# Eight of the 31 taps of one convolution chunk computed on GpSimd instead of VectorE, in a fused decoder-layer kernel

## The reference

```
h = rms_norm(x, g_pre_mix) * (1 + sc1) + sh1
proj = h @ w_in                                  # (2048, 1024) @ (1024, 3072)
cv, cg, q, f, i, g = split(proj)                 # 512 columns each
y_conv = conv_module(cv, cg, ...)                # below
y_rec  = hgrn2(q, f, i, g, ...)                  # chunkwise gated recurrence
x = x + gt1 * rms_norm(concat(y_conv, y_rec) @ w_out, g_post_mix)
... then the router, 32 experts (top 2 of one group) and a second residual

def conv_module(val, gate, dw_kernel, dw_bias, ln_gain, ln_bias):
    u = val * sigmoid(gate)
    u = depthwise causal conv, width 31 (u, dw_kernel) + dw_bias
    return silu(layer_norm(u, ln_gain, ln_bias))
```

## Time and profile before

| | us |
|---|---|
| median of 3 runs (1734.64, 1740.06, 1742.0) | 1740.06 |
| the profiled execution | 1742.48 |
| its span, first to last instruction | 1740.4 |
| mixer: the four blocks and their steps | about 0 to 1115 |
| projections of blocks 1, 2, 3 | about 341 to 478, 581 to 718, 823 to 960 |

### The profile page before, as it was taken

The page is one execution under the profiler, slowest core; times in us unless marked ns, Lnnn a source line. Parts: engine busy times, 40 slices in busy tenths (PEclk is TensorE's granted clock), DMA queues, the critical chain, the costliest instruction groups (busy, mean ns, idle before and its releaser), DMA issues. The chain is left out here.

```text
span 1740.4 us, 23975 instructions
## 1 busy us (share of the span) xinstructions
PE 1536.9 (88%) x7445; PEld 1164.5 (67%) x7446; DVE 1245.5 (72%) x1981; ACT 857.4 (49%) x1495; POOL 380.8 (22%) x401
## 2 busy tenths in 40 slices
PE   2699987999999999999999999459899999999950
PEld 2589975688946789766889565346576666677630
DVE  4589666469885498965598844486678877877828
ACT  2323262333384423563233523216678778878835
POOL 1000000100001000011000011234366666666630
PEclk9999867999999999999999998659899999999985
DMA  9342334233233332332331323637999998789859
GB/s 330 110 145 97 97 121 170 73 85 97 86 109 98 92 98 89 121 105 78 85 97 50 133 85 97 190 127 231 347 324 316 318 330 253 221 248 315 257 107 361
DMA packets 200421, 291.25 MB, mean 167 GB/s; under 512 B 10559, under 2 KB 158172, under 8 KB 200347
## 3 DMA queue, kind: packets, MB, share of 16 engines
q1 hardware_dynamic: 170720, 197.15, 33.9%
q0 software_dynamic: 29360, 92.99, 19.3%
q10 hardware_dynamic: 266, 0.14, 0.0%
HBM read 240.42 MB, written 59.26 MB: 172 GB/s over the span
## 5 line engine op out<-in xcount | busy, mean ns | idle before, releaser
L930 DVE SCALAR_TENSOR_TENSOR cv<-u,taps,cv 128x512 f32<-128x512 f32 x480 | 321.8, 747 | 0.1
L1757 DVE TENSOR_TENSOR w_rest<-wgu,w_high 128x1024 fp32r<-128x1024 f32 x192 | 233.9, 1223 | 95.1 <-ACT w_high L1682 92.5
L1682 ACT ACTIVATE w_high<-wgu 128x1024 fp32r x192 | 201.4, 1054 | 140.0 <-PE pgu L1632 81.4
L484 PE MATMUL bank<-wo,yT 128*128 128x512 f32 x512 | 227.7, 601 | 2.5 <-ACT hT L660 2.5
L457 PE MATMUL bank<-hT_high,tiles_operand 128*128 128x512 f32 x512 | 201.2, 393 | 9.8 <-DVE hT_operand L903 8.5
L458 PE MATMUL bank<-hT_operand,tiles_operand 128*128 128x512 f32 x512 | 200.3, 391 | 0.0
L459 PE MATMUL bank<-hT_high,win_operand 128*128 128x512 f32 x512 | 200.2, 391 | 0.0
L484 PEld LDWEIGHTS bank<-wo,yT 128*128 128x128 f32 x512 | 97.1, 193 | 118.8 <-issue 118.8
L1642 PE MATMUL py<-wd,hTe 128*128 x384 | 172.6, 592 | 0.9 <-ACT yb L1709 0.9
L1630 PE MATMUL pgu<-w_high,x_high 128*128 128x512 f32 x384 | 155.4, 405 | 0.0
L1631 PE MATMUL pgu<-w_rest,x_high 128*128 128x512 f32 x384 | 151.1, 393 | 0.0
(11 more groups left out here) (330 smaller groups left out, 2873.8 us busy)
## 6 DMA issues: line engine op xcount, KB each, us to landing
win<-w_in_in SPq DMA_DIRECT2D x64, 512.0 KB, 5.1
wgu<-w_gate_in SPq DMA_DIRECT2D x32, 1024.0 KB
wgu<-w_up_in SPq DMA_DIRECT2D x32, 1024.0 KB
wd<-w_down_in SPq DMA_DIRECT2D x32, 1024.0 KB
win<-w_in_in SPq DMA_DIRECT2D x16, 1024.0 KB, 5.1
wo<-w_ada_in POOLq DMA_DIRECT2D x6, 2048.0 KB, 9.8
y_dram<-zeros POOLq DMA_DIRECT2D x17, 512.0 KB, 5.1
tiles<-x_in POOLq DMA_DIRECT2D x16, 512.0 KB, 5.8
```

The costliest lines, as they stand in the source:

```text
L484: last = nc.tensor.matmul(out[:], yT[:, w % 2, k, :], wo[:, k, half * 512:(half + 1) * 512], start=(k == 0), stop=(k == KD - 1))
L930: ins = V.scalar_tensor_tensor(out=cv[:, j], in0=u[:, j, w:w + T], scalar=tap, in1=cv[:, j], op0=ALU.mult, op1=ALU.add)
L1682: A(w_high[:, QK * q:QK * q + QK, :], c.wgu[:, bass.ds(slot, 1), QK * q:QK * q + QK, :].rearrange("p a k n -> p (a k) n"), ACT.Copy).then_ ...
L1757: V.tensor_tensor(w_rest[:, part, :], c.wgu[:, bass.ds(slot, 1), part, :].rearrange("p a k n -> p (a k) n"), w_high[:, part, :].bitcast(F3 ...
```

## The change

In the last chunk (j = 3) the taps w = 23 to 30, eight of its 31, are taken out of DVE's stream. POOL computes their sum into `tmp` in a new function `side_taps`: the first tap as a `tensor_scalar` into `tmp`, each of the other seven as a `tensor_scalar` into `scr` and a `tensor_tensor` add of `scr` into `tmp`. That is 15 POOL instructions a block, each waiting on `side_step` for the one before. They begin when all four chunks of this block's `u` are ready. At the end of `conv` DVE waits for `side_step` and adds `tmp` to chunk 3 of `cv`.

```
+        SIDE, SIDE_STEPS = 8, 15
+        CONV_STEPS, MASK_STEPS = NCH * CW - SIDE + 1 + 2 * NCH, 10
...
+            def side_taps(t):
+
+                ch = Chain(pool, side_step, t * SIDE_STEPS)
+                pool.wait_ge(u_ready, (t + 1) * NCH)
+                wait(pool, o_ms, t * NT)
+                wait(pool, dstate_ready, t * 2 * NT)
+                for w in range(CW - SIDE, CW):
+                    tap = c.taps[:, (NCH - 1) * CW + w:(NCH - 1) * CW + w + 1]
+                    out = tmp[:] if w == CW - SIDE else scr[:, 0:T]
+                    ch.link(nc.gpsimd.tensor_scalar(out, u[:, NCH - 1, w:w + T], tap, None, ALU.mult))
+                    if w > CW - SIDE:
+                        ch.link(nc.gpsimd.tensor_tensor(tmp[:], tmp[:], scr[:, 0:T], ALU.add))
+                assert ch.n == SIDE_STEPS
...
             load_ada(pool, 8)
+            side_taps(0)
             for n, p in enumerate((9, 4, 5)):
...
             for t in range(NB + 1):
+                if 0 < t < NB:
+                    side_taps(t)
                 store(t, [w for w in range(NT) if present("y", (w,), t)])
...
                         for j in pair:
+                            if j == NCH - 1 and w >= CW - SIDE:
+                                continue
...
                 taps((2, 3), 17, CW)
-                ch.sync()
+                dve.wait_ge(side_step, (t + 1) * SIDE_STEPS)
+                dve.wait_ge(conv_step, done[NCH - 1])
+                ch.link(V.tensor_tensor(cv[:, NCH - 1], cv[:, NCH - 1], tmp[:], ALU.add))
```

More of the change, by code:

```diff
@@ L154, in mixer_phase @@
         hT_raw, hT_split, high_ready, rest_ready = (sem("hT_raw0"), sem("hT_raw1")), sem("hT_split"), sem("high_ready"), sem("rest_ready")
-        proj_ready = sem("proj_ready")
+        proj_ready, side_step = sem("proj_ready"), sem("side_step")
         gate_sig, u_ready = sem("gate_sig"), sem("u_ready")
@@ L173, in mixer_phase @@
             sem(n) for n in ("conv_step", "q_gated", "ke_ready", "y_normed", "diff_ready"))
-        CONV_STEPS, MASK_STEPS = NCH * CW + 2 * NCH, 10
+        SIDE, SIDE_STEPS = 8, 15
+        CONV_STEPS, MASK_STEPS = NCH * CW - SIDE + 1 + 2 * NCH, 10
         block = ctx.enter_context(nc.Block())
```

## The result

| | before | after |
|---|---|---|
| median | 1741.03 us (4 runs, 1734.64 to 1747.23) | 1780.1 us (4 runs, 1771.02 to 1784.34) |
| the profiled execution's span | 1740.4 us | 1769.3 us |

The ratio is 1.0218, 95% interval 1.0163 to 1.0273: 2.2% slower, about 39 us. The forecast was 1787 in a range from 1753 to 1814, with a chance of 0.87 for slower. The profiled execution of after is the shortest of its four.

The account below looks back on a forecast made before the run. PE was taken to bound the mixer. DVE's loss of 14.1 us a block, less 2.25 (2.38 in block 0) absorbed, gives 47.3 us, minus 0 gain: 1789.8 from the profiled execution, 1787 against the median; range 1753 to 1814.

Parts of the forecast that it names:

- The bound and the two gates: In the projections PE bounds; DVE reaches it through each piece's split and the convolution's end; 2.25 us of delay is absorbed.
- the 6.20 us of idle time: DVE's idle time ahead of piece 10's split in block 2: no cushion, since DVE caused it one round trip earlier.
- The gate of block 0: In block 0 the narrowest late gate was taken to be the split of piece 8, with 2.38 us to spare.
- The gain of 0: At the convolution's end DVE saves 3.7 us, but ACT and DMA hold that place: 0 to 0.3 us a block, taken as 0.
- The loss: POOL's instructions exclude DVE's taps: 8 x 0.74 + 7 x 1.17, so DVE loses 14.1 us in a block.
- The one-input term: Hold of one POOL tensor_scalar of 512 columns, from a selection's row at 1.45 ns a column: 0.74 us, eight a block.
- PE's waits of 11 to 12 us a block: Expected sign in the projections of the profile after: PE waiting on DVE's split of a piece, 11 to 12 us a block.
- The cycle: One POOL hold and one or two taps in turn; 15 take 24 to 34 us, all before the head gates.
- rival (a): DVE keeps the port, POOL advances only in DVE's idle spots, and DVE waits at the add: 15 us, 1755; chance 0.13.
- Rival (b): Taps are exempt from contention and POOL runs beside DVE: 1739 to 1740, not slower; chance 0.11.
- Rival (c), the clock: PE standing in pieces 6 to 10 may drop to 1.2 GHz: up to some 15 us more, 1800; no separate chance.
- My 47: Predicted standing PE over all four blocks: 35.6 us in blocks 1 to 3 plus 11.7 in block 0, 47.3 us.

Follow-up runs that it names:

- the runs with 2 and 4 taps: The changed kernel with GpSimd taking only the last 2 or 4 taps of chunk 3 instead of 8: 1743.32 us and 1749.0 us.
- the VectorE-only kernel: The kernel before with 16 more taps in VectorE's stream, written to tiles nobody reads, GpSimd idle as before: 1774.01 us.
- the kernel with fills: Against the kernel before, VectorE keeps all taps and GpSimd does 15 fills a block that read nothing, instead of arithmetic: 1739.63 us.
- the last experiment: Against the kernel before, VectorE keeps all taps and GpSimd's 15 added instructions a block are all tensor_scalar, results unused: 1757.84 us.
- the first experiment: Against the kernel before, VectorE keeps all 31 taps, GpSimd does its 15 instructions a block and its sum is thrown away: 1776.37 us.

## Why the prediction was right, and where its sizes were off

**The bound and the two gates** held. PE's waits stand at splits of pieces, and the cushion of 2.25 us, made of two idle spots and 0.58 us ahead of piece 10, is what the runs with 2 and 4 taps bracket in blocks 1 to 3: 1.9 us of loss is free, 4.8 us costs 2.3 a block. Reading the 6.20 us of idle time as an echo and not as room was the step that carried the sum. Taken as room, it would have set 8.5 us against 10.8 of loss, and left about 2.3 us a block instead of the 8.4 that PE was late at piece 10. The gate of block 0 was misread: not piece 8 with 2.38 us, but piece 6 with 0.93 and piece 7 with 1.65. With all the loss ahead of piece 7, that is 0.7 us more in the sum.

**The gain of 0** held. DVE's 3.7 us showed as a wait for ACT, 5.11 us in the changed kernel and 3.98 with the taps left out, and the kernel with all taps back on DVE was no slower (1776.4 and 1780.1).

**The loss** had the right mechanism and the wrong size. I took 8 x 0.74 + 7 x 1.17 = 14.1 us; it is 8 x 0.43 + 7 x 1.03 = 10.7. The two-input term was near. The one-input term was taken from the length of a selection, less a fixed part; but a `tensor_scalar` takes 1.56 us alone and holds a tap for only 0.43, so its length says nothing of it. The nearer number would have been the fill's, 0.84 ns a column, times 512: 0.43 us, but only the runs show that. With both measured terms the sum is 10.7 x 4 - 9.1 = 34 us. PE's waits of 11 to 12 us a block, which were named as a sign, were 6 in block 2: 8.4 by this smaller loss, and a part of it went into slow work instead of waiting (below).

**The cycle** was right, 24 to 34 us for the 15: they took 645.85 to 674.95, 29 us. That is also the end of rival (a). POOL gets in at the next change-over between two DVE instructions (its longest two in block 2, 2.93 and 3.48 us, had met a split), and nobody waits at the add. Rival (b), exempt taps, fell with the first tap of 1.78 us.

**Rival (c), the clock,** is a real part, not an alternative. The windows of the changed kernel around the waits for pieces 6 and 10:

```profile
664.00:668.60 4.60, 2.14 (x10) 1.44 (x8) 4.60 (x4) 2.40 (x2) 4.42 (x3) 1.00 0.27 69
668.60:672.00 3.40, 3.35 (x8) 2.68 (x9) 3.40 (x4) 0.00 (x0) 3.22 (x3) 0.50 0.62 215
716.00:719.10 3.10, 0.00 (x0) 0.00 (x0) 2.29 (x2) 3.10 (x4) 0.00 (x0) 1.00 0.59 166
719.80:723.20 3.40, 3.40 (x18) 3.40 (x18) 3.40 (x6) 1.05 (x1) 0.00 (x0) 0.50 0.36 90
```

Behind each of the two waits the granted clock falls to the lower level (0.50, 1.2 GHz) for about 3.4 us; nothing of the kind stood in block 2's projection before. A PE that works through 3.4 us at half speed is late by 1.7. The first time this costs nothing: PE is stopped again at piece 10 until DVE's split is there, and it is as late there (8.39 us) as DVE's lateness alone makes it. Waits shown in block 2 are 2.50 + 0.34 + 3.23 = 6.1 us, less than that, and the rest is slow work. The second time it adds: from the first matmul of piece 10 to the end of the projection PE takes 22.92 us before and 24.50 now, 1.58 more.

So the profiled pair divides like this. In blocks 1 to 3 PE is 25.1 us late up to piece 10 (8.38, 8.39 and 8.37), and 5.7 us later behind it (2.52, 1.58 and 1.59), which is the clock. Block 0 adds 7.6, with both in it. Together that is the 38.5 us of the projections: about 33 from the lateness and about 6 from the clock, with block 0 not divided. My 47 was too high by 3.4 us a block for the one-input and two-input terms, too low by 0.7 for block 0 and by some 6 for the clock, which I had left out of the sum. That 1787 came within 7 us of 1780.1 is partly luck, since these errors point opposite ways.

The profiled pair differs by only 29 us. Up to the first `iota` of the routing it is 1146.03 - 1116.90 = 29.1 us, and in the VectorE-only kernel 1146.14. The 38.5 us are in it, but the stretches between and behind the projections were 9.7 us shorter in the profile of the changed kernel, 7.2 of it behind the last one (156.69 us at a mean clock of 0.91 before, 149.45 at 0.96 now). This stretch varies without regard to the change: 149.5 us in the kernel with fills and 156.4 in the last experiment.

## What to carry to other kernels

Before work is moved to GpSimd beside VectorE, ask two things: does VectorE's work there have two SBUF inputs, and does GpSimd's read SBUF? If both, each such GpSimd instruction takes time from VectorE, here 0.43 us with one input and 1.03 with two, 10.7 us to relieve it of 3.7; fills were free. And count as room only idle time that the late engine has not caused itself: follow what ended it one round trip back.

## What the hardware showed that I had not expected

- A GpSimd `tensor_scalar` of 128x512 float32 takes 1.56 us alone, longer than a `tensor_tensor` (1.29 us), yet costs a VectorE neighbour 0.43 us against 1.03.
- Fifteen fills in a row beside the taps changed neither side: 527 and 746 ns, as alone.
- The two engines take turns at the change-overs between instructions, with a stable cycle of three taps to two GpSimd instructions, 3.46 us, in each of the blocks.
- In the changed kernel, waits of PE of 2.5 and 3.2 us inside an otherwise full stretch of blocks 1 to 3 were each followed by 3.4 us or more at the lower clock. The wait does not decide it alone: in the first experiment the wait of 3.22 us in block 3 was followed by the full clock, and that projection took 145.4 us instead of 146.9; of three waits of 2.3 us with four taps, one was followed by the lower clock.
